# Attention scores as one-pass products of split operands in a one-core diffusion block

## The reference

```python
def block(i):                       # 128 queries; keys of the blocks i-1, i, i+1 and of the context
    s_band = jnp.einsum('bqkgd,bskd->bkgqs', qb, kb) * ATT_SCALE
    s_band = jnp.where(valid, s_band, NEG_INF)              # |k_pos - q_pos| <= 128
    s_ctx = jnp.einsum('bqkgd,bckd->bkgqc', qb, kc) * ATT_SCALE
    p = softmax(concatenate([s_sink, s_ctx, s_band]))       # sink logit, 256 context, 384 local keys
    return p_ctx @ vc + p_band @ vb
```

## Time and profile before

| | |
|---|---|
| median of 3 runs | 2460.81 us (2457.3 to 2463.26) |
| profiled execution, its own time | 2460.81 us |
| its span, first to last instruction | 2459.0 us |
| mean granted clock of PE | 0.968 |
| PE busy | 2237.8 us (91%) |
| PEld busy | 1526.1 us (62%) |
| DVE busy | 1340.5 us (55%) |
| ACT busy | 1150.6 us (47%) |
| POOL busy | 515.3 us (21%) |
| attention stage | from about 1000 to 1575 us of the span |

### The profile page before, as it was taken

The page is one execution under the profiler, slowest core; times in us unless marked ns, Lnnn a source line. Parts: engine busy times, 40 slices in busy tenths (PEclk is TensorE's granted clock), DMA queues, the critical chain, the costliest instruction groups (busy, mean ns, idle before and its releaser), DMA issues. The chain is left out here.

```text
span 2459.0 us, 42927 instructions
## 1 busy us (share of the span) xinstructions
PE 2237.8 (91%) x15061; PEld 1526.1 (62%) x15062; DVE 1340.5 (55%) x2309; ACT 1150.6 (47%) x2065; POOL 515.3 (21%) x842
## 2 busy tenths in 40 slices
PE   5998999999989998799999999489889999898997
PEld 2336777888756665466666666356556666556665
DVE  4456785332335554645565555456466656455774
ACT  4656221122234443545555554255455656455663
POOL 2671110000011010002222222321222222223221
PEclk8999999999989998999999999689999999999999
DMA  8994222221383444412222122568788997777994
GB/s 295 310 267 108 56 56 77 78 69 52 95 217 96 116 104 126 127 52 78 67 76 75 56 69 95 212 212 285 258 284 289 332 311 246 250 227 252 323 303 132
DMA packets 241968, 414.01 MB, mean 168 GB/s; under 512 B 25571, under 2 KB 129259, under 8 KB 236771
## 3 DMA queue, kind: packets, MB, share of 16 engines
q1 hardware_dynamic: 197904, 354.24, 43.8%
q0 software_dynamic: 18800, 44.71, 7.9%
q10 hardware_dynamic: 25125, 13.18, 2.0%
HBM read 344.83 MB, written 76.85 MB: 171 GB/s over the span
## 5 line engine op out<-in xcount | busy, mean ns | idle before, releaser
L937 PE MATMUL ps_proj<-sb_hTh,sb_winh 128*128 128x512 f32 x576 | 234.0, 406 | 5.4 <-DVE sb_hTl L1089 2.7
L2848 PE MATMUL ps_byp<-sb_w,sb_gT 128*128 128x512 f32 x512 | 235.1, 602 | 3.2 <-ACT sb_gT L2655 3.2
L939 PE MATMUL ps_proj<-sb_hTh,sb_winl 128*128 128x512 f32 x576 | 225.3, 391 | 0.0
L938 PE MATMUL ps_proj<-sb_hTl,sb_winh 128*128 128x512 f32 x576 | 224.8, 390 | 0.0
L2848 PEld LDWEIGHTS ps_byp<-sb_w,sb_gT 128*128 128x128 f32 x512 | 93.0, 192 | 97.8 <-issue 92.7
L2237 DVE CUSTOM_DVE_ANT_0 sb_lead<-ps_S,sb_mask 128x640 f32<-128x640 f32 x124 | 102.1, 823 | 87.9 <-PE ps_S L1966 82.0
L2120 ACT ACTIVATE sb_lead<-sb_lead,sb_nm 128x640 f32<-128x640 f32 x128 | 106.3, 830 | 79.4 <-DVE sb_nm L2241 70.9
L1062 ACT COPY sb_rope_or_conv<-ps_proj 128x512 f32<-128x512 f32 x48 | 28.3, 589 | 219.1 <-PE ps_proj L939 144.9
L937 PEld LDWEIGHTS ps_proj<-sb_hTh,sb_winh 128*128 128x128 f32 x576 | 108.6, 189 | 33.4 <-issue 4.1
L938 PEld LDWEIGHTS ps_proj<-sb_hTl,sb_winh 128*128 128x128 f32 x576 | 108.7, 189 | 25.6 <-issue 4.1
L2114 ACT COPY sb_lead<-ps_PT 128x512 f32<-128x512 f32 x160 | 89.3, 580 | 74.3 <-PE ps_PT L1958 74.3
(11 more groups left out here) (344 smaller groups left out, 5398.8 us busy)
## 6 DMA issues: line engine op xcount, KB each, us to landing
sb_lead<-in_exp_w SPq DMA_DIRECT2D x32, 2048.0 KB, 12.1
sb_w<-in_exp_w SPq DMA_DIRECT2D x32, 2048.0 KB, 8.4
sb_raw<-in_exp_w SPq DMA_DIRECT2D x32, 2048.0 KB, 12.5
sb_ada<-in_ada_w SPq DMA_DIRECT2D x16, 1536.0 KB, 8.0
scr_filt<-sb_fout SPq DMA_DIRECT2D x128, 128.0 KB, 3.1
sb_yh<-scr_filt SPq DMA_DIRECT2D x64, 256.0 KB, 5.0
scr_hy_in<-sb_hcT ACTq DMA_DIRECT2D x12, 1024.0 KB, 5.5
sb_win<-in_w_in SPq DMA_DIRECT2D x9, 1024.0 KB, 6.1
```

What stands on the lines that cost most here:

```text
L937: pe.matmul(mp[:, r % 4, 0:N], a, high[:, k, :], start=(k == 0), stop=False)
L938: pe.matmul(mp[:, r % 4, 0:N], a, low[:, k, :], start=False, stop=False)
L939: ins = pe.matmul(mp[:, r % 4, 0:N], b, high[:, k, :], start=False, stop=(k == KT - 1))
L2848: ins = pe.matmul(yp[:, part, :], gT[:, f, :], w2[par][:, f, part * 512:(part + 1) * 512], start=(f == 0), stop=(f == FT - 1), skip_group_ ...
```

## The change

Keys and queries are each split into a high part (rounded to fp32r) and the rest. The tile of keys holds the high part on partitions 0 to 63 and the low part on 64 to 127, for context and local keys in one row of 2560 columns. Queries' high part lies on both halves, the low part on partitions 0 to 63. A score is then two products that add up: 128 rows (query high with key high and key low) and 64 rows (query low with key high), each in one pass. The keys are split in `stage4` in five pieces (ACT copies, DVE subtracts, in jobs 2 to 6), the first tile's queries at the end of that stage, all later queries inside `stage5`: SP loads them three tiles ahead into one buffer, ACT makes the high part after the sinks' exponential, DVE the low part after `sb_mix`. Step -1 does that twice, for tile 1 in the middle of the heads and for tile 2 at its end. `pt` shrinks from 40 blocks to a ring of 32, x2 and xn have one buffer each instead of two, and the mask is stored without a gap between its variants.

```diff
+        kh = e.sb(st, "key_high", [P, 1024], F32R)
...
-            for dst, src in ((g.kT[0:HD, :, P:P + T], g.k_dram), (g.kT[HD:2 * HD, :, 0:C], g.kc_dram),
+            for dst, src in ((g.kT_raw[0:HD, :, C + P:C + P + T], g.k_dram), (g.kT_raw[0:HD, :, 0:C], g.kc_dram),
+                             (g.kT_raw[HD:2 * HD, :, C + P:C + P + T], g.k_dram), (g.kT_raw[HD:2 * HD, :, 0:C], g.kc_dram),
                              (g.v[:, 0:2, :], g.v_dram[:, NT:NT + 2, :]), (g.v[:, 3:3 + NT, :], g.v_dram[:, 0:NT, :])):
...
-                sp.dma_start(g.qb0[part, :, :], g.q_dram[0:1].rearrange("a d h t -> (a d) h t")).then_inc(ld_att, 16)
-            keys = i["mask"].rearrange("p (a k) -> p a k", a=3)
-            sp.dma_start(g.mask[:, :, 0:C + 3 * P], keys).then_inc(ld_att, 16)
-            sp.dma_start(g.mask[:, :, C + 3 * P:], keys[:, :, 0:C]).then_inc(ld_att, 16)
+                sp.dma_start(g.q0_raw[part, :, :], g.q_dram[0:1].rearrange("a d h t -> (a d) h t")).then_inc(ld_q0, 16)
+            sp.dma_start(g.mask[:, 0:3 * (C + 3 * P)], i["mask"]).then_inc(ld_att, 16)
+            sp.dma_start(g.mask[:, 3 * (C + 3 * P):], i["mask"][:, 0:C]).then_inc(ld_att, 16)
...
+            def keys_high(c):
+                if c == 0:
+                    act.wait_ge(ld_kv, 16 * 6)
+                    act.wait_ge(padded, 4)
+                else:
+                    act.wait_ge(k_lo, c)
+                cs = slice(1024 * c, 1024 * (c + 1))
+                act.copy(kh[HD:2 * HD, :], flat(g.kT_raw)[HD:2 * HD, cs]).then_inc(k_hi, 1)
+                act.copy(flat(g.kT)[0:HD, cs], flat(g.kT_raw)[0:HD, cs])
...
+                if j == NJ - 1:
+                    act.wait_ge(ld_q0, 32)
+                    act.copy(g.qh0[:, :, :], g.q0_raw[:, :, :]).then_inc(q_hi, 1)
...
+                if 0 <= j - FIRST_KEYS < KEY_PIECES:
+                    c = j - FIRST_KEYS
+                    cs = slice(1024 * c, 1024 * (c + 1))
+                    ve.wait_ge(k_hi, c + 1)
+                    ve.tensor_tensor(flat(g.kT)[HD:2 * HD, cs], flat(g.kT_raw)[HD:2 * HD, cs], kh[HD:2 * HD, :].bitcast(F32),
+                                     ALU.subtract).then_inc(k_lo, 1)
...
+                    ve.wait_ge(q_hi, 1)
+                    ve.tensor_tensor(g.ql0[0:HD, :, :], g.q0_raw[0:HD, :, :], g.qh0[0:HD, :, :].bitcast(F32), ALU.subtract)
...
-        qb = [g.qb0, e.sb(st, "qb1", [2 * HD, NH, P])]
-        pr = g.lead[:, 0:NH * KEYS].rearrange("p (h k) -> p h k", h=NH)
-        pt = g.lead[:, NH * KEYS:2 * NH * KEYS].rearrange("p (a t) -> p a t", t=P)
+        q_raw = e.sb(st, "q_raw", [2 * HD, NH, P])
+        AT = NH * KEYS
+        pr = g.lead[:, 0:AT].rearrange("p (h k) -> p h k", h=NH)
+        pt = g.lead[:, AT:AT + 32 * P].rearrange("p (a t) -> p a t", t=P)
+        qh = [g.qh0, e.sb(st, "qh1", [2 * HD, NH, P], F32R)]
+        ql = [g.ql0, g.ql1]
...
-        x2 = [e.sb(st, f"x2_{b}", [P, D]) for b in range(2)]
-        xn = [e.sb(st, f"xn2_{b}", [P, D]) for b in range(2)]
+        x2 = e.sb(st, "x2", [P, D])
+        xn = e.sb(st, "xn2", [P, D])
...
+        place_of = [12 + 4 * c if c < 5 else 4 * (c - 5) for c in range(10)]
...
-                def queries():
-                    b = t.back(-2)
-                    wait(sp, qk, 8 * (b.n - 1))
+                def queries(b):
+                    wait(sp, q_lo, b.n - 1)
                     for part in (slice(0, HD), slice(HD, 2 * HD)):
-                        sp.dma_start(qb[b.par][part, :, :], g.q_dram[b.n:b.n + 1].rearrange("a d h t -> (a d) h t"))\
-                          .then_inc(ld_q[b.par], 16)
-                if t.n + 2 < NT and t.n:
-                    queries()
+                        sp.dma_start(q_raw[part, :, :], g.q_dram[b.n:b.n + 1].rearrange("a d h t -> (a d) h t")).then_inc(ld_q, 16)
+                if t.n == -1:
+                    queries(t.back(-2))
+                elif t.n and t.n + 3 < NT:
+                    queries(t.back(-3))
...
-                if t.n == 0:
-                    queries()
+                    sp.dma_start(g.xn_dram[bass.ds(b.n * P, P), :], xn[:, :]).then_inc(st_x[b.par], 16)
+                if t.n == -1:
+                    queries(t.back(-3))
+                elif t.n == 0:
+                    queries(t.back(-3))
...
+                def product(out, tile, p, keys):
+                    h = order[p]
+                    pe.matmul(out, qh[tile.par][:, h, :], g.kT[:, h // 4, keys], start=True, stop=False)
+                    return pe.matmul(out, ql[tile.par][0:HD, h, :], g.kT[0:HD, h // 4, keys], start=False, stop=True)
+
                 def local(tile, p):
                     if p == 0 and tile.n:
-                        pe.wait_ge(ld_q[tile.par], 32 * (tile.half + tile.par))
-                    return pe.matmul(mixer_local if tile.n == 0 and p % 2 else local_of[p % 2], qb[tile.par][0:HD, order[p], :],
-                                     g.kT[0:HD, order[p] // 4, bass.ds(tile.n * P, 3 * P)], start=True, stop=True)
+                        pe.wait_ge(q_lo, tile.n)
+                    return product(mixer_local if tile.n == 0 and p % 2 else local_of[p % 2], tile, p,
+                                   slice(C + tile.n * P, C + (tile.n + 3) * P))
...
-                        context = pe.matmul(mixer_context if alone and p % 2 else context_of[p % 2], qb[nx.par][HD:2 * HD, order[p], :],
-                                            g.kT[HD:2 * HD, order[p] // 4, 0:C], start=True, stop=True)
+                        context = product(mixer_context if alone and p % 2 else context_of[p % 2], nx, p, slice(0, C))
...
-                            x = pt[:, :, :].rearrange("p (h k a) t -> p k a h t", h=4, k=2)[:, kv, a, 2 * half:2 * half + 2, :]
+                            x = pt[:, 12 - 12 * half:32 - 12 * half, :].rearrange("p (h k a) t -> p k a h t", h=2, k=2)[:, kv, a, :, :]
...
+                            if c == 8:
+                                act.wait_ge(pv, 2 * t.n + 1)
                             act.wait_ge(tp, 10 * t.n + c + 1)
-                            act.copy(pt[:, 4 * c:4 * c + 4, :].rearrange("p a t -> p (a t)"), PT[:, (t.par + c) % 2, :])\
+                            act.copy(pt[:, place_of[c]:place_of[c] + 4, :].rearrange("p a t -> p (a t)"), PT[:, (t.par + c) % 2, :])\
...
+                def queries_high(b):
+                    act.wait_ge(ld_q, 32 * b.n)
+                    wait(act, qk, 8 * (b.n - 1))
+                    act.copy(qh[b.par][:, :, :], q_raw[:, :, :]).then_inc(q_hi, 1)
...
                 head(1)
                 head(2)
+                if t.n == -1:
+                    queries_high(t.back(-2))
                 head(3)
                 head(4)
...
                     act.activation(esk[:, nx.par, :], esk[:, nx.par, :], ACT.Exp).then_inc(eso, 1)
+                if t.n + 3 < NT:
+                    queries_high(t.back(-3))
...
+                def queries_low(b):
+                    ve.wait_ge(q_hi, b.n)
+                    if b.n == 1:
+                        ve.wait_ge(filled, 16)
+                    ve.tensor_tensor(ql[b.par][0:HD, :, :], q_raw[0:HD, :, :], qh[b.par][0:HD, :, :].bitcast(F32),
+                                     ALU.subtract).then_inc(q_lo, 1)
...
-                    wait(ve, st_x[pj.par], 32 * pj.half)
+                    if pj.n:
+                        ve.wait_ge(st_x[pj.back(1).par], 32 * (pj.back(1).half + 1))
                     do(residual(pj, 0))
...
+                if t.n == -1:
+                    queries_low(t.back(-2))
...
+                if t.n + 3 < NT:
+                    queries_low(t.back(-3))
                 if project:
                     first_half()
...
-        g.kT = att.enter_context(nc.sbuf_tensor("sb_kT", [2 * HD, NKV, T + 2 * P], F32, side="right"))
+        with nc.sbuf_tensor("sb_kT_raw", [2 * HD, NKV, C + T + 2 * P], F32, side="right") as g.kT_raw:
+            pass
+        g.kT = att.enter_context(nc.sbuf_tensor("sb_kT", [2 * HD, NKV, C + T + 2 * P], F32R, side="right"))
```

More of the change, by code:

```diff
@@ L1243, in stage4 @@
         ld_att = e.sem("s4_attention_inputs_loaded")
+        ld_q0 = e.sem("s4_first_queries_loaded")
+        k_hi = e.sem("s4_keys_high")
+        k_lo = e.sem("s4_keys_low")
+        q_hi = e.sem("s4_first_queries_high")
         e.sems["hyena_last_tile_stored"] = g.last_hyena_tile
@@ L1246, in stage4, with flat @@
         block = st.enter_context(nc.Block(no_gpsimd_drain=True))
+        FIRST_KEYS, KEY_PIECES = 2, NKV * (C + T + 2 * P) // 1024
+        def flat(keys):
+            return keys[:, :, :].rearrange("p a t -> p (a t)")
         def inverse_view(b):
@@ L1705, in stage5 @@
         last_router = S[:, 1024:1024 + P]
-        mask_of = [slice(C, KEYS + C), slice(0, KEYS)]
+        mask_of = [[mask[:, v * KEYS + at:(v + 1) * KEYS + at] for v in range(3)] for at in (C, 0)]
+        place_of = [12 + 4 * c if c < 5 else 4 * (c - 5) for c in range(10)]
```

(26 more changed lines are left out.)

25 lines of the change are left out of this document (14 added, 11 removed).

## The result

The changed kernel takes 2510.34 us in the median of 4 runs (2501.53 to 2512.82), the kernel before beside it 2459.85 us: a ratio of 1.0197, 95% interval 1.0182 to 1.0212. The direction was forecast; the time of 2489 us was 21 us too low, and the result lies outside the range of 2440 to 2504.

What follows compares the result with a forecast made beforehand. The prediction took PE, busy 91% of the span, to bound the kernel. Terms of 1.5 + 5 + 0.5 + 2 + 19.5 = 28.5 us on 2460.8 us gave 2489 us, with an 8-in-10 range of 2440 to 2504.

Steps and rivals of the forecast that it cites:

- Changes of shape: Stage 5 scores: four array shape changes a head instead of two, losing 0.19 or 0.16 us each; a head 0.28 us longer.
- The rival of free changes: Stage 5 scores: shape changes cost fp32r nothing and weight loads stay hidden; 2438 us in all, chance 0.18.
- Steps at 2.4 GHz: Stage 5, steps 2 to 14 at full clock: 1.5 us more a step, 19.5 us over 13 steps.
- The clock in the steps: Stage 5, steps 2 to 14: granted clock taken to stay at 2.4 GHz, so no time added.
- The main case: Whole kernel: shape changes cost their full loss, 2489 us with its own range of 2478 to 2502, chance 0.66.
- a case with falls: Stage 5 steps: granted clock falls in every step, up to 1.5 us each, 20 us in all; 2509 us, chance 0.07.
- Starts in step -1: Stage 5, step -1: late queries and slower score products delay the next step's first mask by 5 us, bounds 2 and 9.
- The queries' part: Step -1: uncovered splitting and late loading of queries make the next step's first mask 3.8 us late.
- The PE part: Step -1: a head's scores on PE take 1.28 us against DVE's 1.03, partly at the lower clock: 1.2 us more.
- The table's transfer: Step -1: DVE's subtraction of queries waits for the filled table's transfer and ends 2.1 us late.
- Step 1: Stage 5, step 1: same cost as later steps, with some passes at the lower clock: 2 us.
- Stage 4: Key splitting covered by idle time; the first tile's queries at the end not covered, 1.5 us later.

Runs made afterwards that it cites:

- the other execution: The changed kernel executed once more with no edit: 2513.09 us, ratio 1.0229 to the kernel before.
- slow DVE: Against the kernel whose low products take all 128 rows, a useless DVE addition of 128x512 before each mask: 2531.1 us in the profiled execution.
- kernel with old products: The changed kernel, but each score is again one full f32 product on 64 rows, leaving out part of the operands: 2451.92 us, ratio 0.9975.
- kernel with 128 rows: The changed kernel with low products on all 128 rows, so no score product changes shape: 2436.27 us, ratio 0.9911 to the kernel before.
- either order: Two edits of the changed kernel: both high products before both low, 2479.82 us; or high products on 64 rows too, 2458.29 us.

## Why the prediction was off

Point by point, by its own steps.

Changes of shape: right. Forecast 0.19 us on the way to 64 rows and 0.16 on the way back; measured 0.19 to 0.20 both ways. From a head's first score pass to the transposes or values behind it that was to be 1.28 us (1.39 less the transpose ahead) and is 1.35. The rival of free changes is refuted in the changed kernel, yet its numbers were good: with the changes taken out, 31.85 us a step (forecast 31.8) and 2436 us (2438). The rule of "TensorEngine Tiling (Array Packing)" in the Trainium skill, section Key Properties, that a change of tiling mode drains the engine, agrees with these rows, both where changes stand (0.19 us) and where they don't (0.12 and 0.17 for streaming alone).

Steps at 2.4 GHz: 35.55 us, 1.85 more than before, forecast 1.5. The four heads that PE bounds gave 4 x 0.33 = 1.3 (forecast 1.12); the other 0.5 (forecast 0.4) is left for the first four, by difference. PE's marked waits for masks, 0.27 in the third head before and 5.0 us in 300 us of these steps, are gone altogether, as forecast. 13 x 1.85 = 24 us, forecast 19.5.

The clock in the steps: this is the step that failed. The main case took 2.4 GHz in steps 2 to 14 for granted, since the earlier trace rows show it before, and put the term at nothing. It gave a case with falls 0.07, "against it: the shape changes are short". They are short, but 32 a step. In the profiled execution the clock was at 1.2 GHz for 34 us of these steps, and they took 14.6 us more than the 24 above; in the other execution 41 us and 17. Without these 14.6 us the result would be about 2496, inside the range. The rival had forecast 20 us for this, with a fall in every step; 8 and 10 of the 13 had one. That the measured 2510 us comes so close to its 2509 is in part luck: it put the clock 3 to 5 us too high and shared the main case's terms for the starts and the steps, which were some 7 and 4.5 us too low, while the shorter end took 4.6 off. The slow DVE shows that falls come without any change of shape between the scores. That in the changed kernel the lost 0.19 us each lower the clock is the likely reading, since no step from 2 to 14 has a fall with two changes a head or fewer. What exactly brings a fall wasn't measured.

Starts in step -1: forecast 5 us and 0.5 for step 0, measured 12.1 (13.7 between the means of two executions each). The first mask of tile 1 comes 10.2 us later, forecast about 5. The queries' part, forecast 3.8 us, is 4.2 at that mask in the kernel with old products, and 5 to 7 at the first values. The PE part, forecast 1.2 us as "partly at the lower clock", is 7 to 9: all eight heads of tile 0 ran at 1.2 GHz, and there a change costs 0.30 us instead of 0.19. This follows from rows: 0.50 to 0.52 and 0.62 us between passes above, 0.21 and 0.32 in the kernel with 128 rows at the same clock. So a head takes 2.26 us, not 1.28, and over eight heads that is 8 us. The table's transfer, 2.1 us in the forecast, cost nothing here, since PE's beat had moved the fifth mask to 1016.46; that term would have been real only with faster scores, as in the kernel with 128 rows.

Step 1: forecast 2, measured 2.7 (3.9 in the second execution, against the mean of before). Stage 4: 1.5 forecast; 1.4 to 5.8 measured, with a spread of its own over the kernels. The ring, the buffers, the queries' split inside the steps: 0 forecast, 0 measured (33.72 us steps with the old products).

Summed: forecast 28.5 us, measured 52.0 between the profiled executions; of the 23.5 us between, 14.6 are the clock's falls in steps 2 to 14, about 7 steps -1 and 0, 4.5 the undisturbed steps, and 2 step 1 and the time up to the first score product; the shorter end takes 4.6 off.

What stays open: why the clock is at 1.2 GHz for 37 and 40 us of steps -1 and 0 in the two executions of the changed kernel, and for 8 and 5 us in the kernel before. The other kernels, whatever their products, have 14 to 33 us there, in no clear order, and 38 us with the slow DVE in the same steps. The queries' part at the start is hardly larger than the spread of these steps between executions (3.4 us in the kernel with 128 rows). And why 5 and 3 of the changed kernel's 13 steps, with the same products, had no fall isn't shown.

## What to carry to other kernels

Count the array's shape changes (rows or columns in use) in the order in which PE gets its products, price each at the 0.19 us measured here at 2.4 GHz, and look for an operand that can be filled up instead: here the low product on 128 rows cost no time and turned a kernel 2% slower than the one before into one 0.9% faster. When a change makes PE stand more often without moving less, forecast the clock too: find a stretch of the trace where products come as thinly, and read its granted clock, over several steps, since here some fell and some did not. At 1.2 GHz reckon the fixed losses at the lower clock as well, not the streaming alone.

## What was not expected of the hardware

The loss at a change of shape grows at the lower clock, from 0.19 to 0.30 us. It did not depend on where in the head the changes stood: 1.37 us for two changes in either order. The weight load, which takes 0.19 us and otherwise runs ahead of its product, starts with its product there. PE's busy share hides it all: 100% in a window whose products are 5% fewer than in the kernel before, and 100% while the clock falls. Steps 2 to 14 of 34.1 us and less kept 2.4 GHz in every kernel, while the slowed kernel's, 36.7 to 38.6 us with their falls, never did.
